# Split matrix products with the moving operand read from its last column to its first

## What is computed

```python
for l in range(DEPTH):                       # first network
    h = x @ w_in[l]                          # 256 x 1024 by 1024 x 7328
    ...
    x = _layernorm(DEEPNORM_ALPHA * x + merged @ w_out[l], ln1_g[l], ln1_b[l])
    f = jnp.square(jax.nn.relu(x @ mlp_w1[l])) @ mlp_w2[l]
    x = _layernorm(DEEPNORM_ALPHA * x + f, ln2_g[l], ln2_b[l])
for l in range(DEPTH):                       # second network
    u = _rmsnorm(h, norm_mix_g[l])
    (s_z, s_xbc, ...) = _split(u @ w_in[l], IN_SIZES_2)
    ...
    up = _dwconv(u @ w_up[l], ffn_conv_w[l], ffn_conv_b[l])
    h = h + (jax.nn.silu(a_half) * v_half) @ w_down[l]
    h = h + (p[l] @ w_ple[l]) * jax.nn.sigmoid(h @ w_ple_gate[l])
```

## Time and profile before

| what | before |
|---|---|
| median of three runs | 2486.16 us |
| the profiled execution | 2493.97 us |
| its span, first to last instruction | 2492.2 us |
| TensorE busy | 2440.8 us, 98% |
| VectorE busy | 1786.6 us, 72% |
| ScalarE busy | 1452.0 us, 58% |
| GpSimd busy | 291.6 us, 12% |
| mean granted TensorE clock | 0.994 |
| DMA | 430.5 MB, 173 GB/s |

### The profile page before, as it was taken

How to read it: one execution, slowest core, us unless ns; L and a number is a source line. 1 busy time by engine, 2 the same in 40 slices (tenths; PEclk the granted TensorE clock), 3 DMA queues, 4 the chain that set the end, 5 groups by cost and what they waited for, 6 DMA issues and landing times.

```text
span 2492.2 us, 43110 instructions
## 1 busy us (share of the span) xinstructions
PE 2440.8 (98%) x17744; PEld 2232.4 (90%) x17744; DVE 1786.6 (72%) x2889; ACT 1452.0 (58%) x2130; POOL 291.6 (12%) x222
## 2 busy tenths in 40 slices
PE   8999999999999999899999999999999999999998
PEld 8888999988889899799999799998898999899996
DVE  4567675565576755669867887885599768887875
ACT  5547555445466455467665655664667656656654
POOL 0000002000000000002222720000012207500000
PEclk9999999999999999899999999999999999999999
DMA  7554476555544565555566655566554567645663
GB/s 248 157 145 118 154 247 193 186 185 168 140 125 142 173 201 186 168 158 144 145 178 186 194 153 192 187 192 197 149 161 135 162 191 197 184 148 190 189 210 127
DMA packets 358920, 430.50 MB, mean 173 GB/s; under 512 B 20616, under 2 KB 286310, under 8 KB 358468
## 3 DMA queue, kind: packets, MB, share of 16 engines
q1 hardware_dynamic: 341312, 401.72, 53.1%
q10 hardware_dynamic: 14340, 14.93, 2.7%
q0 software_dynamic: 3072, 11.10, 1.5%
HBM read 424.44 MB, written 3.24 MB: 172 GB/s over the span
## 4 chain that ended last, share of the span: by engine, by line
PE 87%; DVE 9%; ACT 2%; issue 1%; DMA 1%; ACTq 0%; POOL 0%; POOLq 0%; DVEq 0%
PE ps L112 85%; PE ps L115 2%; DVE wlo L121 2%; DVE sE L121 1%; DVE hgA L148 1%; DVE hgQF L121 0%; DVE hgQB L121 0%; ACT lnv L118 0%; DVE hgkf L121 0%; DVE hgkb L121 0%; DMA kT<-in_diff_lambda 0%; DVE sbc L130 0%; DVE sE L124 0%; DMA memN<-in_mem 0%; DVE hgTf L121 0%
## 5 line engine op out<-in xcount | busy, mean ns | idle before, releaser
L121 DVE TENSOR_TENSOR wlo<-wring,whi 128x1024 fp32r<-128x1024 f32 (+1 forms) x768 | 919.2, 1217 | 252.7 <-ACT whi L118 252.1
L118 ACT ACTIVATE whi<-wring 128x1024 fp32r<-128x1024 f32 (+1 forms) x768 | 803.5, 1054 | 427.9 <-PE ps L112 415.8
L112 PE MATMUL ps<-uT,whi 128*128 128x256 f32 x4640 | 817.8, 280 | 6.1 <-DVE wlo L121 4.5
L112 PEld LDWEIGHTS ps<-uT,whi 128*128 128x128 f32 x4640 | 705.8, 188 | 16.4 <-DVE wlo L121 7.5
L112 PE MATMUL ps<-uT,wlo 128*128 128x256 f32 x2320 | 645.4, 278 | 0.0
L112 PEld LDWEIGHTS ps<-uT,wlo 128*128 128x128 f32 x2320 | 436.1, 188 | 0.0
L112 PE MATMUL ps<-xT,whi 128*128 128x256 f32 x2112 | 381.0, 284 | 2.9 <-DVE xT L121 1.7
L112 PEld LDWEIGHTS ps<-xT,whi 128*128 128x128 f32 x2112 | 323.4, 188 | 9.7 <-issue 5.6
L112 PE MATMUL ps<-xT,wlo 128*128 128x256 f32 x1056 | 296.4, 281 | 0.0
L112 PE MATMUL ps<-whi,hid 128*128 128x512 f32 x864 | 270.4, 392 | 0.0
L112 PEld LDWEIGHTS ps<-xT,wlo 128*128 128x128 f32 x1056 | 199.4, 189 | 0.3
(11 more groups left out here) (400 smaller groups left out, 3576.9 us busy)
## 6 DMA issues: line engine op xcount, KB each, us to landing
wring<-in_w_in SPq DMA_DIRECT2D x346, 512.0 KB, 4.2
wring<-in_mlp_w SPq DMA_DIRECT2D x128, 512.0 KB, 4.4
wring<-in_w_up SPq DMA_DIRECT2D x88, 512.0 KB, 4.5
wring<-in_w_down SPq DMA_DIRECT2D x44, 512.0 KB, 4.5
wring<-in_w_branch SPq DMA_DIRECT2D x32, 512.0 KB, 3.4
wring<-in_w_out SPq DMA_DIRECT2D x32, 512.0 KB, 4.6
wring<-in_mem_w_kv SPq DMA_DIRECT2D x16, 512.0 KB, 5.9
wring<-in_w_br_hg SPq DMA_DIRECT2D x16, 512.0 KB, 4.6
```

The lines of the kernel that those rows point to most:

```text
L112: return self.e.matmul(*p, **k) if self.e else Nothing()
L118: return self.e.activation(*p, **k) if self.e else Nothing()
L121: return self.e.tensor_tensor(*p, **k) if self.e else Nothing()
```

## The change

The moving operand and the output of all six matmuls in `tokens` and `features` are given with their columns reversed. Column j of the moving operand still lands in column j of the output; the order in which the columns are read, and written, runs from the last to the first. The stationary operand, the number and order of instructions, the tiles and their places, the waits and the signals are what they were: each engine has the same list of instructions before and after (on TensorE 10541 rows that group equal neighbours, the same in both).

```diff
@@ tokens
             for k in range(p.nk):
                 e.wait_ge(*at((x.name, q0 + k)))
                 xh, xl = x.at(q0 + k, t * 128, 128)
-                e.matmul(o, xh, p.hi[:, k, :], start=first and k == 0, stop=False)
-                e.matmul(o, xh, p.lo[:, k, :], start=False, stop=False)
-                m = e.matmul(o, xl, p.hi[:, k, :], start=False, stop=fin and k == p.nk - 1)
+                e.matmul(o[:, ::-1], xh, p.hi[:, k, ::-1], start=first and k == 0, stop=False)
+                e.matmul(o[:, ::-1], xh, p.lo[:, k, ::-1], start=False, stop=False)
+                m = e.matmul(o[:, ::-1], xl, p.hi[:, k, ::-1], start=False, stop=fin and k == p.nk - 1)
             m.then_inc(*up("pe_panel", ("panel", p.i, t)))
@@ features
                 ch, cl = p.hi[:, k, j0:j0 + w], p.lo[:, k, j0:j0 + w]
-                e.matmul(o, ch, xh, start=q == 0 and j0 == 0, stop=False, skip_group_check=True)
-                e.matmul(o, ch, xl, start=False, stop=False, skip_group_check=True)
-                m = e.matmul(o, cl, xh, start=False, stop=q == chunks - 1, skip_group_check=True)
+                e.matmul(o[:, ::-1], ch, xh[:, ::-1], start=q == 0 and j0 == 0, stop=False, skip_group_check=True)
+                e.matmul(o[:, ::-1], ch, xl[:, ::-1], start=False, stop=False, skip_group_check=True)
+                m = e.matmul(o[:, ::-1], cl, xh[:, ::-1], start=False, stop=q == chunks - 1, skip_group_check=True)
         m.then_inc(*up("pe_panel", ("panel", p.i, 1)))
```

## The result

The changed kernel takes 2536.1 us, the median of four runs (2534.29 to 2536.27), against 2486.8 us for the kernel before, to which a fourth run has come (2485.28 to 2489.66): a ratio of 1.0186 with a 95% interval of 1.0166 to 1.0205. It is **slower by 49 us**. The time lies in the stated range, but the forecast was no change, and that was wrong.

A forecast was written before the change was run, and what follows sets the result against it. TensorE, busy 98% of the span, was taken to bound the kernel. The profiled 2493.97 us plus 0 for the reversal, with the runs' median 7.8 us lower, gave 2486 us; range 2320 to 2650.

The forecast's parts named there:

- What bounds the kernel: TensorE, busy 98% of the span, sets the end time; how long products hold it goes straight in.
- the list of edits at no cost: Instruction lists, semaphores, DMAs, queues and waits on banks stay as they are in all engines: 0 us.
- the bounds: Backward columns in split products: 0.4167 ns each, 161 us less, up to 0.833 ns each, 1805 us more.
- The nearest rows: Same split products forwards at full clock, 0.4427 ns per column, taken for the backward read: no change, chance 0.32.
- the SBUF half of the rule: SBUF reads: 16-byte lines, full performance on hits to the same line; four hits either way, so no change.
- Rival 2: Split products: backward read meets the next stationary load every time; long pitch (117.9, 233.3 ns) everywhere, +38 us, 2524 us; 0.20.
- further term: Backward reads of split products: the loss per 64 bytes also doubles, 123 us more, 2647 us.
- Rival 1: Split products: the loss per product goes away, short pitch everywhere; 38 us less, 2448 us; chance 0.22.
- rival 3: Split products: reading or writing neighbours in pairs needs rising addresses; half pace, 1805 us more, 4291 us; chance 0.19.
- Its sign: TensorE timeline: any product of 256 columns above 118 ns at full clock would show half pace.
- Rival 4: Split products: backward read loses no cycle per 64-byte block; the whole 161 us goes, 2325 us; chance 0.07.
- one cycle lost for every 16 columns: Short forward pitch of split products: 6.6 and 13.4 ns above one column per cycle, in proportion to moving columns.

The follow-up runs named there:

- e3_read: Changed kernel with outputs written forwards again, moving operand still read backwards: 2534.45 us, 1.0173 to the kernel before.
- e4_write: Kernel before with outputs of all split products written backwards, reads forwards: 2490.18 us, 1.0005.
- e10_narrow_back: Against the kernel before: reads backwards, and split products between first and last of an accumulation load 32 stationary columns instead of 128: 2532.19 us.
- base 0: Arena moved to a multiple of 128 bytes instead of 64 past one: changed kernel 2554.91 us (1.0284), kernel before 2533.51 us (1.0190).

## Why the prediction was wrong

**What bounds the kernel** was right: TensorE's pitch goes straight into the end time. The pitches of the changed products add up to 49 us, against 46 us by the ratio and 49 by the medians. VectorE and ScalarE kept their busy time and waited more for TensorE, so no other engine took part, as the list of edits at no cost had it.

**The step that failed** is the choice inside the bounds: "The nearest rows are those of the same products forwards at the same clock", and from it no change. A term of the sum, what the direction of the read costs, was put at nothing. It measured 2.95 ns per product of 256 columns and 4.25 per product of 512, 35 + 14 us, and `e3_read` and `e4_write` show that the read has all of it. The bounds themselves, 161 us less and 1805 us more, held. But the forward row was taken as a value when all it could give was a neighbour, and no row held a descending read. That the same columns, and so the same bytes, are touched in both directions is true and did not settle it: by the SBUF half of the rule of the Trainium skill (Advanced Engine Details and Errata, section Memory Cachelines), as the prediction read it (a line is hit four times either way), the sum stays as it is, and the trace does not agree: up to 6.7 ns more per product.

**Rival 2** had the sign and nearly the size: the long pitch everywhere, 2524 us, against 2536. It got the pitches of 117.9 and 233.3 right and not the 120.0 ns of some stretches. Its cause was wrong. It made the loss a collision with the stationary load; `e10_narrow_back` took three quarters of that load away and the loss stayed. That the time lies in the range is therefore luck in part: it lies near rival 2's number, and not for rival 2's reason. Its further term, a second cycle per 64 bytes with pitches of about 120 and 240 ns and 123 us more, did not come: 120 is there in some stretches, but 512 columns never left 233.3 at this base. On base 0 they reach 236.7 in about half of the stretches, which no part of the prediction explains.

**Rival 1** and **rival 3** fell as they were framed: no stretch kept 113.3 ns, and nothing came near 213. Rival 3 had hung on pairs of neighbours, on the write side too, and `e4_write` shows that the write side is free. Its sign, any 256-column product above 118 ns, was set too near: the stretches at 120.0 passed it, and nothing ran at half pace.

**Rival 4** had a slip in its sum: its 161 us is the whole distance to one column per cycle, and 38 us of that is the loss per product; the loss per 64 bytes alone is the 123 us of rival 2. Rival 4, and with it "one cycle lost for every 16 columns", misread the forward pitch. That rate gives 128 columns 56.7 ns, 384 columns 170.0; measured were 59.4 and 173.1. What fits the forward rows of the table within 0.6 ns, 192 columns in their better stretches among them, is one column per cycle plus one step of 6.7 ns for each 256 columns begun: 60.0, 86.7, 106.7, 113.3, 173.3, 200.0 and 226.7. It was found from these rows and gives the shortest pitch at each width, no more: 90.0 at 192, 117.8 at 256, 202.7 at 448 and 228.9 at 512 are as steady in other stretches. At the two widths of this kernel the two laws give the same numbers, so its trace alone could not tell them apart. And the gain that rival 4 hoped for in features isn't there: the load holds a product at 111.7 ns, 1.6 ns under the short pitch.

**The chances.** 0.39 for slower against 0.32 for the same: the single case was put above a larger heap. With the pitch known to come in steps, and 0.33 ns per product enough to leave "no change", the likeliest case was too narrow to be the forecast.

## What to carry to other kernels

Read the moving operand of a float32r product from low to high addresses; if an order has to be turned round, turn the output, which cost nothing here (1.0005, 0.9989 to 1.0021). Where such products come back to back, compare pitches with the sum "columns per cycle, plus a step of 6.7 ns per 256 columns begun, but no less than the load of the next stationary operand (111.7 ns for 128 columns)" as a lower end, and vary the width before trusting a law read from one or two widths. Read the pitch over the whole trace, not in one stretch: one and the same kernel has two or three steady pitches at one width. The placement of operands can be worth as much as such a change: 64 bytes of it were 46 us here, and most of that was gone with narrow loads.

## What had not been expected

- With 128 stationary columns of float32r, a product has a pitch of 111.7 ns however few columns it moves (128, 192 or 224), so at 256 columns, 113.3 ns, load and moving read are within 2% of each other. With 32 stationary columns 128 moving ones take 59.4 ns.
- Less load made 512-column products slower on the whole: a mean of 231.7 instead of 229.1 ns forwards. Why stays open.
- One backward product in three slows its two forward neighbours at 256 columns, and at 512 columns where the forward kernel is at 228.9 ns, but not where it is at 226.7.
- What makes the step for a backward read, and why it is smaller at some widths than at others, stays open. A stationary operand read backwards was not tried.
